# A decoder step with expert lookup: new TensorE costs and fetch waits in the planner, and the ranking placed ahead of the next attention

## The reference

```
z = rms_norm(x) @ w_in                 # 1024 -> 2304, heads of 64
mixer A: 8 query heads on 2 key heads, window of 128, with a sink
mixer B: 8 heads, three dilated windows, joined by their softmax weights
x = x + [norm_a(A) ++ norm_b(B)] @ w_out
h = rms_norm(x)
q = (h @ w_q) as 8 heads x 2 halves x 128
s1, i1 = top16(q[:, 0] @ keys[0].T);  s2, i2 = top16(q[:, 1] @ keys[1].T)
top_s, pos = top16(all 256 sums s1 + s2);  eid = i1*128 + i2 at pos
act = gelu(h . u[eid]) * softmax(top_s)    # 8 heads x 16 experts a row
x = x + sum(act * v[eid]);  y = rms_norm(x)
```

## Time and profile before

| what | before |
|---|---|
| median of 3 runs | 3883.09 us |
| profiled execution | 3865.63 us |
| its span, first to last instruction | 3863.8 us |
| TensorE busy | 2715.3 us (70%) |
| VectorE busy | 2532.2 us (66%) |
| ScalarE busy | 631.4 us (16%) |
| GpSimd busy, which issues the gathers | 2339.2 us (61%) |
| transfers | 1295.70 MB, mean 335 GB/s |
| granted TensorE clock, mean | 0.839 of full |

### The profile page before, as it was taken

How to read it: one execution, slowest core, us unless ns; L and a number is a source line. 1 busy time by engine, 2 the same in 40 slices (tenths; PEclk the granted TensorE clock), 3 DMA queues, 4 the chain that set the end, 5 groups by cost and what they waited for, 6 DMA issues and landing times.

```text
span 3863.8 us, 30640 instructions
## 1 busy us (share of the span) xinstructions
PE 2715.3 (70%) x7286; PEld 1323.9 (34%) x7286; DVE 2532.2 (66%) x6330; ACT 631.4 (16%) x1880; POOL 2339.2 (61%) x2076
## 2 busy tenths in 40 slices
PE   5866669687778777777798785457766566665665
PEld 3533335343434344334344343122332222222221
DVE  1467777677766677767667876555787555555553
ACT  2112212122211121212111121001111011110110
POOL 0155644476465577776745775444667777777774
PEclk7877879788899888888999888678987988888887
DMA  9799889899789899998988998777999999999997
GB/s 365 269 365 335 311 334 345 328 349 347 259 311 357 342 344 357 344 351 316 352 332 300 361 358 311 275 259 259 363 353 354 368 374 367 376 360 377 365 372 251
DMA packets 344554, 1295.70 MB, mean 335 GB/s; under 512 B 41880, under 2 KB 44784, under 8 KB 330912
## 3 DMA queue, kind: packets, MB, share of 16 engines
q0 software_dynamic: 298368, 1086.46, 76.2%
q1 hardware_dynamic: 46008, 207.29, 14.2%
HBM read 1272.76 MB, written 55.43 MB: 344 GB/s over the span
## 4 chain that ended last, share of the span: by engine, by line
POOL 24%; PE 24%; DMA 23%; issue 12%; DVE 9%; DVEq 3%; another core or an unknown queue 2%; ACT 1%; SPq 1%; ACTq 0%; POOLq 0%
DMA v_ring<-in_peer_v,idx 13%; POOL v_ring L1355 12%; POOL u_ring L1350 12%; PE acc L1594 12%; PE pS L1400 4%; DMA u_ring<-in_peer_u,idx 4%; PE pA L1526 3%; DMA wbuf<-zS_scr 2%; DVE u_ring L2204 2%; PE pS L1503 1%; DVE accs L2244 1%; DMA xbuf<-in_x_all 1%; PE pS L1442 1%; DMA o_all<-in_cache_swa 1%
## 5 line engine op out<-in xcount | busy, mean ns | idle before, releaser
L1594 PE MATMUL acc<-v_ring,diag 128*128 128x512 f32 x2820 | 1662.0, 733 | 861.0 <-DMA v_ring<-in_peer_v,idx 728.1
L1355 POOL DMA_INDIRECT v_ring<-in_peer_v,idx x1024 | 1191.3, 1163 | 772.3 <-PE acc L1594 355.4
L2204 DVE CUSTOM_DVE_ANT_0 u_ring<-u_ring,hb 128x1024 f32<-128x1024 f32 x1024 | 1244.7, 1222 | 577.8 <-DMA u_ring<-in_peer_u,idx 554.8
L1350 POOL DMA_INDIRECT u_ring<-in_peer_u,idx x1024 | 1123.5, 1097 | 713.3 <-issue 292.5
L1594 PEld LDWEIGHTS acc<-v_ring,diag 128*128 128x128 f32 x2820 | 605.5, 230 | 1748.6 <-issue 1603.1
L2244 DVE SCALAR_TENSOR_TENSOR accs<-v_ring,wv,accs 128x1024 f32<-128x1024 f32 x319 | 409.8, 1285 | 89.1 <-DMA v_ring<-in_peer_v,idx 57.4
L1832 ACT ACTIVATE diag<-idn,wv 128x128 f32<-128x128 f32 x705 | 264.8, 396 | 1160.1 <-PE acc L1594 818.9
L1400 PE MATMUL pS<-wbuf,T 128*128 128x512 f32 (+1 forms) x640 | 263.5, 562 | 22.7 <-DVE T L1927 16.0
L1526 PE MATMUL pA<-T,wbuf 128*128 128x256 f32 (+2 forms) x1280 | 256.4, 357 | 21.3 <-issue 15.6
L1526 PEld LDWEIGHTS pA<-T,wbuf 128*128 128x128 f32 x1280 | 221.2, 204 | 72.8 <-issue 46.6
L1400 PEld LDWEIGHTS pS<-wbuf,T 128*128 128x128 f32 x640 | 123.0, 197 | 142.7 <-issue 129.5
(11 more groups left out here) (224 smaller groups left out, 1908.4 us busy)
## 6 DMA issues: line engine op xcount, KB each, us to landing
wbuf<-in_w_in SPq DMA_DIRECT2D x40, 1024.0 KB
wbuf<-in_w_q SPq DMA_DIRECT2D x40, 1024.0 KB
out_dil_s<-in_cache_dil SPq DMA_DIRECT2D x8, 4092.0 KB
wbuf<-in_w_out SPq DMA_DIRECT2D x20, 1024.0 KB
u_ring<-in_peer_u,idx POOLq DMA_INDIRECT x1024
v_ring<-in_peer_v,idx POOLq DMA_INDIRECT x1024
xbuf<-in_x_all SPq DMA_DIRECT2D x16, 512.0 KB
wbuf<-in_w_in SPq DMA_DIRECT2D x10, 512.0 KB
```

The source lines that it names most:

```text
L1350: pool.indirect_dma_start(u_ring[:, entry % RU, :], None, table, bass.IndirectOffsetOnAxis(rows, 0))\
L1355: pool.indirect_dma_start(v_ring[:, entry % RV, :], None, peer_v, bass.IndirectOffsetOnAxis(rows, 0))\
L1594: m = pe.matmul(acc[0:R, half * 512:(half + 1) * 512], w, v_ring[:, entry % RV, half * 512:(half + 1) * 512], start=first, stop=last, skip ...
L2204: dve.tensor_tensor_reduce(row, row, hb[:, t % 2, :], 1.0, 0.0, ALU.mult, ALU.add, dots[:, section % 2, j:j + 1]).then_inc(u_used, 1)
```

## The change

`times_of` gets lower costs for nearly all stages on TensorE, and the planner's cost of one weighing on TensorE falls from 1.98 to 1.25. `merged` advances the second queue of a phase 1.8 times slower than the first, so that the ranking ends when 5/9 of the other queue's work is done. The planner delays a `smul` or `spv` step until 12 us after the step before it that frees the buffer. Its due places now stand for every head of a tile, not for the first alone. It holds `r3` until the tile that last used the slot of `idx` has ended. The rest of the diff moves definitions.

```diff
-        return (("PE", 1.9 if a[0] == "kva" else 3.6),)
+        return (("PE", 1.1 if a[0] == "kva" else 2.0),)
...
-        return (("PE", 7.2),)
+        return (("PE", 4.0),)
...
-        "q": (("PE", 3.4 if len(group) == 1 else 4.0),), "qe": (("ACT", 0.36),), "k": (("PE", 0.45 * len(group)),),
+        "q": (("PE", 1.2 if width_of(group) < 2 * P else 2.1),), "qe": (("ACT", 0.36),), "k": (("PE", 0.2 * len(group) + 0.1),),
...
     queues = [list(q) for q in queues]
+    spread = (1.0, SPREAD)
...
-        i = max((i for i, q in enumerate(queues) if q), key=lambda i: work(queues[i]) / total[i])
+        i = max((i for i, q in enumerate(queues) if q), key=lambda i: -(1.0 - work(queues[i]) / total[i]) * spread[i])
...
+SPREAD = 1.8
...
+FETCH = 12.0
...
-            n = self.given[t, 0]
-            if n > marks[-1][0]:
-                marks.append((n, max(p - 10, 1)))
+            for h in range(HEADS if t != SAMPLE else 1):
+                n = self.given[t, h]
+                if n > marks[-1][0]:
+                    marks.append((n, max(p + TOPK * h - 10, 1)))
...
-                out += [("weigh", p, 1.98)] if pick_v(p) is not None else []
+                out += [("weigh", p, 1.25)] if pick_v(p) is not None else []
...
+        if BASE[n][0] in ("smul", "spv") and BASE[n][2] == 0:
+
+            m = n - 1 if BASE[n][0] == "spv" or BASE[n][1] == 0 else AT["smul", BASE[n][1] - 1, 1]
+            if BASE[n][0] == "spv" and BASE[n][1] == 0:
+                m = AT["smul", NS - 1, 1]
+            if BASE[n][0] == "spv" and BASE[n][1] > 0:
+                m = AT["spv", BASE[n][1] - 1, 0]
+            end = self.part_end.get((m, 0))
+            if end is None:
+                return None
+            ready = max(ready, end + FETCH)
+        if BASE[n][0] == "r3":
+
+            for t in BASE[n][6]:
+                if OI[t] >= SLOTS and ("fsum", ORDER[OI[t] - SLOTS]) not in self.ends:
+                    return None
```

More of the change, by code:

```diff
@@ L41 @@
 SC_SLOTS = 4
+SLOTS = 5
+SLOT = {t: i % SLOTS for t, i in OI.items()}
 PLACE_IN_GROUP = {t: s for g in GROUPS for s, t in enumerate(g)}
@@ L68, in rows_of, with width_of @@
     return NS if t == SAMPLE else P
+def width_of(group):
+    return sum(rows_of(t) for t in group)
 def prompt_of(group):
@@ L260, in times_of @@
     return {
-        "xg": (("DVE", 2.7),), "zt": (("PE", 0.5 if a == "kva" else 1.8),),
+        "xg": (("DVE", 2.7),), "zt": (("PE", 0.3 if a == "kva" else 0.8),),
         "zv": (("ACT", 0.35 if a == "kva" else 0.65),),
-        "s": (("PE", 0.8 if first else 0.6 + 0.25 * n),), "sm": (("DVE", 1.9 if first else 1.3 + 0.14 * n),),
-        "se": (("ACT", 1.4 if first else 1.3 + 0.12 * n),), "p": (("PE", 0.9 if first else 0.8 + 0.4 * n),),
-        "pe": (("ACT", 0.5 if first else 0.9 + 0.12 * n),), "v": (("PE", 0.7 if first else 0.7 + 0.3 * n),),
+        "s": (("PE", 0.6 if first else 0.6 + 0.13 * n),), "sm": (("DVE", 1.9 if first else 1.3 + 0.14 * n),),
@@ L266, in times_of @@
+        "se": (("ACT", 1.4 if first else 1.3 + 0.12 * n),), "p": (("PE", 0.6 if first else 0.5 + 0.18 * n),),
+        "pe": (("ACT", 0.5 if first else 0.9 + 0.12 * n),), "v": (("PE", 0.5 if first else 0.5 + 0.14 * n),),
         "vd": (("DVE", 0.6),), "vo": (("ACT", 0.6),),
-        "n1": (("ACT", 1.5),), "n2": (("DVE", 2.9),), "n3": (("ACT", 1.3),), "nt": (("PE", 3.3),), "ng": (("ACT", 2.4),),
+        "n1": (("ACT", 1.5),), "n2": (("DVE", 2.9),), "n3": (("ACT", 1.3),), "nt": (("PE", 1.6),), "ng": (("ACT", 2.4),),
@@ L276, in times_of @@
+        "spe": (("ACT", 1.0),), "spv": (("PE", 2.1),), "sod": (("DVE", 2.0),), "sfo": (("PE", 1.1),),
         "so": (("DVE", 1.3),), "sr0": (("DVE", 3.4),), "sr1": (("DVE", 2.4),), "sr2": (("DVE", 1.5),), "sr3": (("DVE", 2.7),), "sge": (("ACT", 0.3),),
@@ L714 @@
 STAGED = {x: i for i, x in enumerate(x for x in Z_ITEMS if x[0] in ("qa", "qb") and 0 < x[1] < NT)}
-SLOTS = 5
-SLOT = {t: i % SLOTS for t, i in OI.items()}
 R3 = [s for s in BASE if s[0] == "r3"]
 RANKED = {(t, s[2]): i + 1 for i, s in enumerate(R3) for t in s[6]}
-def width_of(group):
-    return sum(rows_of(t) for t in group)
 X_LOADS = (("sq", 0), ("sq", 1), ("sq", 2), ("o", 0), ("sq", 3), ("sq", 4), ("o", 1), ("o", 2), ("sq", 5), ("sq", 6),
```

7 lines of the change are left out of this document (3 added, 4 removed).

## The result

| | before | changed |
|---|---|---|
| median on the first chip | 3878.14 us (4 runs, 3873.05 to 3890.93) | 3923.41 us (4 runs, 3899.91 to 3928.45) |
| profiled execution | 3865.63 us | 3928.45 us |
| TensorE / VectorE busy | 2715.3 / 2532.2 us | 2830.8 / 2441.1 us |

The ratio is 1.0100, with a 95% interval of 1.0051 to 1.0149: slower by 1%, where I had forecast 3825 us, faster by 1.5%. One thing has to be said at once, since it limits this number: on two other chips of the same kind the same two kernels stood at 0.9946 [0.9912, 0.9980] and 0.9966 [0.9942, 0.9989]. The record gives no number of the chip of this result; I call it the first.

What follows compares the result with a forecast made beforehand. The DMA queue was taken to bound, with compute engines deciding how often it runs dry. Terms -36 -3 -55 -11 +8 +49 = -48 gave 3818 from 3865.6, or 3835 from the median; forecast 3825 us, range 3755 to 3905.

Steps and rivals of the forecast that it cites:

- crowding behind the output steps, +49: Behind the two-tile output steps, TensorE work crowds: shortage 35 us per window, 105 for three, less 56 idle now; bounds 0, 120.
- Numbers earlier, -36: In stretch 914 to 1112, expert numbers come earlier, GpSimd's four waits for them go: -36 us.
- Opening, -3: Before the first expert numbers, one narrow projection half and two ropes less: -3 us.
- Sample rows, -55: In stretch 2350 to 2658, late key and value rows lose 65 us; all but 10 recovered: -55 us.
- my residual of 10 us: Part of the sample's 65 us loss taken to remain, since fetches overhang by 0 to 3 us; bounds 0 and 65.
- Rival (b): The sample's rows come late all the same; net -8 to +7, about 3873 us; chance 0.16.
- estimate of 4.5 us: Fetch of a row's keys, 1.09 MB, by the skill's fit; nothing would remain and the sum be 10 us better.
- VectorE relieved, -11 and +8: 74 weighings move to TensorE: stretch 305 to 510 gains 11 us; four heads' rankings crowd the first thirty places, +8.
- Rival (c): TensorE bounds behind the output steps: 183 us a window, +175 instead of +49, net +78, about 3950 us; chance 0.13.
- My sign of three stretches of 60 to 70 us: Behind the output steps, TensorE over 0.95 busy and DMA share 0.75 to 0.85 would show the forecast right.
- late to nobody: Query weights: slots reloaded one head ahead on SyncE's queue; a head's two queries with what is between last over 10 us.
- (d): The change does not do what it says in time, gains and losses cancel: 3883 us; chance 0.06.

Runs made afterwards that it cites:

- old costs and even merging: Changed kernel with all TensorE costs of the kernel before and SPREAD 1.0 for 1.8, leaving the fetch wait and due places: 3707.01 us, ratio 0.9677.
- the fetch wait alone: Kernel before with the planner's 12 us fetch wait; costs, merging and due places as before, hold of `r3` kept: 3755.92 us, ratio 0.9795.
- SPREAD 1.0: Changed kernel with the two queues of a phase merged evenly, factor 1.0 for 1.8, low costs kept: 3908.3 us, ratio 1.0104.
- SyncE's later order: Changed kernel with an output step counted as ended 12 us later for SyncE's order only: 3793.04 us, and 3794.87 us beside the changed kernel, ratio 0.9890 both times.
- first group of experiments: Four edits of the changed kernel where the kernel before takes 3868.73 us: old TensorE costs 3748.01, SPREAD 1.0 3908.3, old weighing cost 3867.72, no fetch wait 3966.49.
- third group: Runs where the kernel before takes 3835.29 us: both repairs 3750.85, old costs with SPREAD 1.0 and SyncE's later order 3729.52, traced costs 3756.6, changed kernel 3811.03.
- the two repairs together: Changed kernel with output steps 12 us later for SyncE's order and old TensorE costs for latent and query projections: 3750.85 us, ratio 0.9777.
- `z` and `q` alone: Changed kernel with old TensorE costs for the latent and query projections only (1.9/3.6 and 3.4/4.0): 3772.02 us, ratio 0.9824, beside the changed kernel.

## Why the prediction was wrong

The step that failed is the term for crowding behind the output steps, +49: in the same places the DMA engines idle 122 us more than before. The sizes below are for the profiled executions on the first chip where they are compared with the terms, and medians elsewhere; where two chips are compared it is said.

**Numbers earlier, -36: right.** The four waits are gone. The due places alone brought 49 us (3755.9 to 3707.0), in a kernel with the old costs and even merging. By the view of stretches, the fetch wait alone:

```profile
165.20:1944.80 1779.60, 1326.58 (x4001) 716.13 (x4000) 1286.24 (x3431) 359.73 (x1074) 1072.14 (x943) 0.85 0.91 339
1944.80:2648.40 703.60, 522.03 (x1380) 248.10 (x1378) 503.01 (x1216) 111.83 (x319) 459.35 (x401) 0.84 0.93 344
```

and with the due places:

```profile
165.20:1929.80 1764.60, 1367.83 (x4169) 736.27 (x4168) 1309.41 (x3548) 362.51 (x1087) 1073.06 (x946) 0.86 0.93 347
...
1929.80:2596.90 667.10, 475.47 (x1210) 220.56 (x1209) 487.97 (x1132) 105.08 (x301) 456.91 (x398) 0.84 0.96 352
```

The first 480 places are only 15 us shorter and the next 200 are 36, but TensorE also does 41 us more in the first and 47 less in the next, so work has moved ahead. Idle DMA time falls from 160 to 124 us in the first (1779.6 x 0.09, 1764.6 x 0.07), which is the 36 of the forecast, and from 49 to 27 in the next, which the forecast did not have.

**Opening, -3.** GpSimd's first wait fell from 161.5 to 154.1 us, and the first dot stands at 160.3 us and not at 166.3: -6. Why it fell is not shown: the first wait is 161 us again both with SPREAD 1.0 (161.1) and with SyncE's later order (161.5).

**Sample rows, -55: right in kind, too small.** The fetch wait alone gives 0.9795, 78 us, and idle DMA time in places 480 to 680 falls from 114 us (the kernel before) to 49; within the changed kernel the wait is worth 58 us. One set of the changed kernel, issued by SyncE:

```profile
2202.41 1.28 SPq L1204 DMA_DIRECT2D wbuf<-in_cache_dil  x3
```

and first used by VectorE:

```profile
2216.88 1.23 DVE L2143 TENSOR_TENSOR wbuf<-wbuf 128x1024 f32<-128x1024 f32 x1 [2.25 <-DMA wbuf<-zS_scr]
```

The fetch takes 14.5 us, as in the earlier trace rows, and VectorE waits for 2.25 of it: my residual of 10 us was 7.4 by the waits. Rival (b) is out. So is the estimate of 4.5 us that I had worked out from the Trainium skill (DMA: Bandwidth & Descriptors, Anatomy of one DMA): the set took 14.5 us in this trace too. I had also stretched the fit that the Trainium skill gives there: it is for one transfer that GpSimd issues, and a set here is six loads that SyncE issues, beside the gathers.

**VectorE relieved, -11 and +8.** The groups by line, which answer to the earlier trace rows:

```profile
L1615 PE MATMUL acc<-v_ring,diag 128*128 128x512 f32 x3116 | 1779.8, 713 | 773.9 <-DMA v_ring<-in_peer_v,idx 681.9 <-issue 50.2 <-ACT diag L1853 40.8
...
L2265 DVE SCALAR_TENSOR_TENSOR accs<-v_ring,wv,accs 128x1024 f32<-128x1024 f32 x245 | 314.9, 1285 | 70.9 <-DMA v_ring<-in_peer_v,idx 46.7 <-issue 11.4
```

VectorE has 74 weighings less, as counted, and is busy 91 us less in all (95 worked out); TensorE 115 more (133 to 227 worked out). No run takes this term by itself. The weighing's old cost, which undoes a third of the shift, made the kernel faster by 1%, but it changed the windows and SyncE's order too, so what the shift itself is worth stays open.

**Crowding, +49: the step that failed.** I had put the idle time of three windows of 20 places at 105 us and taken off the 56 that three stretches idle now. These are the windows in the trace, from the last transposes of h (568.43, 1118.38 and 1712.97) over 20 places:

```profile
568.40:733.70 165.30, 149.49 (x504) 91.74 (x504) 117.62 (x450) 29.46 (x77) 46.40 (x42) 0.92 0.76 265
1118.40:1281.40 163.00, 147.94 (x502) 91.36 (x503) 112.23 (x423) 29.37 (x77) 43.40 (x40) 0.92 0.71 251
1713.00:1861.20 148.20, 136.04 (x428) 70.54 (x429) 99.44 (x381) 20.43 (x53) 36.89 (x37) 0.94 0.69 238
```

The work on TensorE and its pace were right: I had counted 141 us for the second, and TensorE is busy 149, 148 and 136. Rival (c) had 183 for such a window, a factor of 1.3, and that is not there; the 181 to 186 us of the longer windows further above are over thirty places. So (c) came near the time by another way than its own. My sign of three stretches of 60 to 70 us did not fit my own 141 either.

Three things made the term too small. In these windows TensorE also stands still for 13.1, 12.1 and 10.0 us on a load of rotated queries (`qT<-qT_scr`), which the count left out; they last 476 us and idle 165.3 x 0.24 + 163.0 x 0.29 + 148.2 x 0.31 = 133, not 105: 28 more. Ahead of the last transposes, where VectorE waits for residual rows, the thirty places idle 63.6 x 0.10 + 55.8 x 0.12 + 54.2 x 0.23 = 26 more. I had looked at where TensorE's own work was moved, and not at how a wrong cost moves SyncE's queue: of the query weights the prediction says that they are late to nobody, of the residual load it says nothing. And the 56 that I took off belong to stretches of 207, 218 and 191 us; the same thirty places of the kernel before idle 40: 16 more. With my 49, and 3 for windows that do not end at the same places, that is the 122.

That the low costs do it is shown by the first group of experiments: on one chip the windows idle 178 us with them and 17 with the old ones, 161 us, and the kernels are 160 us apart.

**The sum.** Table of costs: on the chips of 3869 to 3878 us it is 1.0100 against 0.9675, about +165 us, where my terms for it (+49, -11, +8, and part of -3) made some +45. The rest of the change: -3.25%, about -120 us, where I had -91. So the forecast gains were too small by a quarter, and the measured loss is more than three times mine. On the faster chips the table costs less. On that of the third group the old costs, with even merging and SyncE's later order, are 82 us below the changed kernel beside them (3811.03 to 3729.52), and the two repairs together 60. On that of the fourth, SyncE's order alone is 27 and `z` and `q` alone 50. The 21 us between 82 and 60 are not taken apart, and the intervals of the two kernels overlap. One candidate is a third effect of the low cost of an output step, which neither repair touches: VectorE waits for its halves 63.1 us in 6 with both repairs, and 27.0 in 2 with the old costs.

**The chip.** Neither the forecast nor its rivals had a term for it, so that (d) or (c) comes nearest is in part luck. On the chips of 3832 to 3835 us the changed kernel is 10 and 24 us faster than the kernel before, and rival (d), gains and losses cancel, is nearest. On the first it is 45 slower, between (d) and (c).

## What to carry to other kernels

A cost in a planner's table does not only order the engine it belongs to: whatever is sorted by that clock moves with it, here SyncE's loads, and an in-order queue turns a cost that is 3 us too low into a wait of 22. When such a table changes, compare the order of every queue, and look in each for an instruction with a late condition that has moved ahead of one that others wait for.

Durations that are true for single instructions need not be the best costs: the older costs above the traced ones were 27 us better here, with intervals that overlap a little, and why is not shown. A change in parts of both signs is best taken apart: the parts of this one without its table gave 0.9677.

## What the runs showed of the hardware

- One program differs between chips (or groups of runs, since each had its own chip), and not all programs alike: the kernel before 3878 and 3832 us (1.2%), the changed one 3923 and 3822 (2.6%). The ratio of the two was 1.3% apart on these chips, near three times the half-width of the wider interval. Repairs must be held against a kernel beside them.
- The same gathers of the changed kernel's tail ran at 363 GB/s on the first chip and at 378 on that of the fourth group, at a DMA share of 0.97 and 0.99; those of the kernel before at 364 and 368. Over the whole changed kernel the packets of the two large queues took 3530 us of the engines' time and 3487, for the same bytes; in the kernel before 3493 and 3480.
- The granted clock of TensorE over the whole changed kernel was 0.860 on the first chip and 0.878 on the other, and 0.839 and 0.832 for the kernel before: it did not go with the chip's speed in both.
